# First convolution tap on ScalarE for 512 tokens of a tile, and the carried columns copied at the tile's head

## The chip, the cores and the metric

One core of a Trainium2 chip. The metric is the device time of one execution in microseconds: 3367.95 us, the median of three runs (3359.31, 3367.95 and 3372.1). Engines are called as in the profile: PE is TensorE, DVE is VectorE, ACT is ScalarE, POOL is GpSimd, SP is the queue that issues most DMAs.

## What is computed

One inference step of a decoder layer: projections, a state-space branch, attention over the prompt and over a paged cache, an output projection, and a feed-forward network with a causal depthwise convolution of width 3 on its gate branch. Only the last part matters here. For the 2048 tokens of the prompt:

```
gate = xn @ w_gate                      # 1024 -> 2816 channels
up   = xn @ w_up
padded = concatenate([conv_prev, gate]) # two earlier rows in front
conv = conv_b + sum(padded[:, i:i + t] * conv_w[i] for i in range(3))
hdn  = gelu(conv) * up
x    = x + rmsnorm(hdn @ w_down, g_post_ffn)
```

Eight sample tokens go through the same layer with a convolution state of their own. All data are float32.

## The kernel before, in words

**Tiles.** `stage_ffn` takes 128 of the 2816 channels and 1024 of the 2048 tokens at a time. That is 22 channel tiles for each half of the tokens, 44 tiles, called g = 0 to 43 here; g = 21 is the turn tile, in which the x operands of the second half are loaded and split, and from it on each tile also carries the eight sample tokens (`sample_channels`, `sample_taps`). Tiles 0 to 3 and 20 to 43 are written out; tiles 4 to 19 are a hardware loop of four passes with four tiles each, in which waits and addresses that depend on g go through registers.

**Seven products.** Gate and up for two times 512 tokens would be eight block products; the kernel makes them from seven, as in a Strassen-Winograd scheme, in the order K1, K6, K2, K7, K5, K4, K3. Each product is 12 matmuls of 128x512 (four blocks of x, three terms of a high and low part), so a tile is 84. They go into the PSUM banks A, B and C, and DVE and ACT add them up between: ACT copies K1 (L2852, tile `m1`) and K2 (L2858, into the first 512 tokens of `gbuf`, signal `c11_ready`); DVE makes L3058 after K6, L3063 after K7, L3066 after K5, L3069 after K4 and L3072 after K3. PE's product K7 waits for L3058, K4 for L3063, K3 for L3066. L3072 completes the other 512 tokens of `gbuf`.

**Weights.** For each product of the next tile ACT rounds the weight operand (L2798, `split`) and DVE makes its low part (L2949), both at the same step of the current tile. Four of the operands are sums that POOL makes first (L1736 to L1742). In every second tile of the loop POOL also makes four sums of x parts for the second half (L2642), on data that SP loads behind the stores of the pair.

**The convolution.** `taps` on DVE ends a tile. It copies the two columns carried from the previous token half, which are zeros in the first (L3017, signal `carried`), makes the first tap with the bias over all 1024 tokens (L3028), the two other taps (L3031, twice, signal `tapped`), and saves the last two columns (L3032, signal `saved`). Gelu of a tile (L2809, ACT) and the product with `up` (L2985, DVE) come at step K6 of the next tile. In even tiles DVE then adds the pair up (L2997) for SP to store; `w_down` is applied after the last tile (L2778).

**Order.** Each engine runs its list in the order written. The waits in front of the first tap guard its output `conv`: the stores and sums of the tiles that used that slot before, and in tiles 0 to 3, 22 and 23 the splits of x operands that are staged in the same memory.

Of the kernel before, what the change touches and what calls it, by code (L numbers as in the profile page):

```python
# [18 lines left out]
ALU = mybir.AluOpType  # L19
ACT = mybir.ActivationFunctionType  # L20
# [16 lines left out]
FT = FF // P  # L37
PAGE = 128
NPG = 64
CH = 512  # L40
GRP = 4
QUAD = P // GRP
CW = 3
ROWS = NS * (CW - 1) + CW + 1
TAP, BIAS = NS * (CW - 1), ROWS - 1
# [5 lines left out]
KH = KD // 2  # L51
OPS = 7
K1, K6, K2, K7, K5, K4, K3 = range(OPS)
# [2178 lines left out]
def stage_ffn(nc, A, keep, early):  # L2232

    with ExitStack() as ctx:
# [4 lines left out]
        PASS = 2 * CH  # L2239
# [61 lines left out]
        def xop(k, h):  # L2301
# [27 lines left out]
        sd_used, sd_upper, sd_summed, sd_placed = m.sem("sd_used"), m.sem("sd_upper"), m.sem("sd_summed"), m.sem("sd_placed")  # L2329
        s_squared, s_mean, s_r, s_scaled, s_y, s_x1, s_stored = (  # L2330
            m.sem(n) for n in ("s_squared", "s_mean", "s_r", "s_scaled", "s_y", "s_x1", "s_stored"))
        waited = m.sem("waited")

        def tiles(eng, body):

# [8 lines left out]
        def known(g, low, high=LASTG):  # L2344

            return isinstance(g, int) and low <= g < high

        def at(eng, sem, n):

            if not isinstance(n, int) or n > 0:  # L2350
                eng.wait_ge(sem, n)
# [66 lines left out]
        with nc.Block() as block:  # L2418
# [371 lines left out]
            def _(act):  # L2790
# [49 lines left out]
                def body(g, f, j, h2):  # L2840
                    s = j % 2
                    turn = known(g, FT - 1, FT)
                    sampled = known(g, FT - 1, LASTG - 1)
                    last = known(g, LASTG - 1)
                    for k in range(OPS):
                        if k == K1:
                            act.wait_ge(prod, g * OPS + k + 1)
                            at(act, c21_ready, g)
                            if known(g, 0, 1):
                                act.wait_ge(x_t4, 1)  # L2850
                                act.wait_ge(x_ready[K6], 1)
                            act.activation(m1, bank[:, 3 * s + A_B, :], ACT.Copy).then_inc(m1_ready, 1)  # L2852
                            if known(g, 0, 1):
                                split_q(K4, 2, x_t4, 1)
                        if k == K2:
                            act.wait_ge(prod, g * OPS + k + 1)
                            at(act, tapped, g * CW)
                            act.activation(gbuf[:, CW - 1:CW - 1 + CH], bank[:, 3 * s + A_B, :], ACT.Copy).then_inc(c11_ready, 1)  # L2858
                        if not last:
                            split(g + 1, k, (j + 1) % 2, h2 + j % 2)  # L2860
                        else:
                            if k == K7:
                                split_a(0)
                            for n in ((0, 1), (2,), (3, 4), (5, 6), (7, 8), (9, 10), ())[k]:
                                split_wd(n)
                            if k == K4:
                                split_a(1)
                        if k == K1 and sampled:
                            x = g - FT + 1
                            act.wait_ge(s_made, x + 1)  # L2870
                            at(act, s_ready, x)
                            act.activation(s_rows[:], bank[:, S_B, 0:2 * P].rearrange("p (q c) -> p q c", q=2), ACT.Copy).then_inc(s_copied, 1)
                        if k == K6 and not known(g, 0, 1):
                            gelu(g - 1, (j - 1) % 4)
                        if k == K5 and sampled:
                            act.wait_ge(s_tapped, (g - FT + 2) * CW)
                            act.activation(small[:], small[:], ACT.Gelu_apprx_tanh).then_inc(s_gelu, 1)
                        if turn:
                            for q in range(KH):
                                split_x(k, q)  # L2880
# [63 lines left out]
            def _(dve):  # L2944
# [67 lines left out]
                def taps(g, f, j, h2):  # L3012
                    one = lambda x: x[:, bass.ds(f, 1)].rearrange("p o n -> p (o n)")
                    p, tl, c = one(prm), one(tails), conv[:, j, :]
                    tap = lambda k: p[:, TAP + k:TAP + k + 1]
                    at(dve, saved, g)
                    ts(gbuf[:, 0:CW - 1], tl[:, 0:CW - 1], 1.0, None, ALU.mult).then_inc(carried, 1)  # L3017
                    dve.wait_ge(carried, g + 1)
                    dve.wait_ge(c11_ready, g + 1)
                    dve.wait_ge(c12_ready, g + 1)  # L3020
                    if not known(g, 0, 4):
                        dve.wait_ge(hraw_stored[j % 2], h2 * 16 - 16)
                        dve.wait_ge(hsummed, h2 * 5 - 5)
                    if known(g, 0, 4):
                        dve.wait_ge(x_ready[K4], 1)
                    if known(g, FT, FT + 2):
                        dve.wait_ge(x_ready[K3], 1 + KH)
                    ts(c, gbuf[:, 0:PASS], tap(0), p[:, BIAS:], ALU.mult, ALU.add).then_inc(tapped, 1)  # L3028
                    for k in (1, 2):
                        dve.wait_ge(tapped, g * CW + k)  # L3030
                        stt(c, gbuf[:, k:k + PASS], tap(k), c, ALU.mult, ALU.add).then_inc(tapped, 1)  # L3031
                    ts(tl[:, 0:CW - 1], gbuf[:, PASS:], 1.0, None, ALU.mult).then_inc(saved, 1)  # L3032
# [12 lines left out]
                def body(g, f, j, h2):  # L3045
                    b = lambda x: bank[:, 3 * (j % 2) + x, :]
                    turn = known(g, FT - 1, FT)
                    sampled = known(g, FT - 1, LASTG - 1)
                    last = known(g, LASTG - 1)
                    t1 = gbuf[:, CW - 1 + CH:]  # L3050
                    for k in range(OPS):
                        if k in (K6, K7, K5, K4, K3):
                            dve.wait_ge(prod, g * OPS + k + 1)
                        if k == K6:
                            dve.wait_ge(m1_ready, g + 1)
                            at(dve, tapped, g * CW)
                            at(dve, saved, g)
                            tt(t1, m1, b(B_B), ALU.add).then_inc(u2_ready, 1)  # L3058
                        if k == K7:
                            at(dve, h_ready, g)  # L3060
                            if known(g, 0, 1):
                                dve.wait_ge(x_t4, 1)
                            tt(up[:, CH:], m1, b(B_B), ALU.add).then_inc(u3_ready, 1)  # L3063
                        if k == K5:
                            dve.wait_ge(u3_ready, g + 1)
                            tt(up[:, CH:], up[:, CH:], b(C_B), ALU.add).then_inc(c22_ready, 1)  # L3066
                        if k == K4:
                            dve.wait_ge(c22_ready, g + 1)
                            tt(up[:, 0:CH], m1, b(B_B), ALU.add).then_inc(c21_ready, 1)  # L3069
                        if k == K3:  # L3070
                            dve.wait_ge(u2_ready, g + 1)
                            tt(t1, t1, b(C_B), ALU.add).then_inc(c12_ready, 1)  # L3072
                            if last:
                                split_wd(9)
                                split_wd(10)
                                split_a(1)
                            taps(g, f, j, h2)
                        if not last:
                            split(g + 1, k, (j + 1) % 2)
                        else:  # L3080
                            for n in ((0,), (1, 2), (3,), (4,), (5, 6), (7, 8), ())[k]:
                                split_wd(n)
                            if k == K5:
                                split_a(0)
                        if k == K6 and not known(g, 0, 1):
                            multiply(g - 1, (j - 1) % 4)
                        if j % 2 == 0 and not known(g, 0, 1):
                            sum_h(g, j, h2, {K2: (0, 1), K7: (2,), K5: (3,), K4: (4,)}.get(k, ()))
                        if k == K7 and sampled:
                            sample_taps(g - FT + 1)  # L3090
                        if k == K4 and sampled:
                            x = g - FT + 1
                            dve.wait_ge(s_gelu, x + 1)
                            tt(hs[:, x, 0:NS], small[:], bank[:, S_B, S_U:S_U + NS], ALU.mult).then_inc(s_h, 1)
                        if turn:
                            for q in range(KH):
                                split_x(k, q)
# [118 lines left out]
```

## Time and profile before

| what | value |
|---|---|
| median of three runs | 3367.95 us |
| the profiled execution: its time, its span | 3369.25 us, 3367.6 us |
| mean granted TensorE clock | 0.966 |
| PE busy over the span | 93% |
| DVE, ACT, POOL busy over the span | 71%, 39%, 28% |
| feed-forward tiles | from 1942 us to 2904 us of the span |

The span is the time from the first to the last instruction. A busy PE is one with matmuls in its pipeline. In the rows, a group of instructions is given by line, engine, operation, output and inputs; in a timeline the time in brackets is how long the engine was idle before it and which instruction ended that.

### The profile page before, as it was taken

To read this page: it belongs to the slowest core of one execution; us is meant where nothing else is said; L and a number is where in the kernel's file an instruction comes from. 1 tells how busy PE (TensorE), PEld (TensorE's weight loads), DVE (VectorE), ACT (ScalarE), POOL (GpSimd) and SP (SyncE) were. 2 spreads that over 40 slices of the span, in tenths; PEclk is the share of its full clock that TensorE was granted. 3 is DMA by queue.
4 is the path that set the end of the run, shared out by engine and by line. 5 is a ranking of instruction groups with operands and counts; after the bars stand their busy time and mean duration, and the time that the engine had idled before them with its cause. 6 is when DMAs were issued, how large, how long until landed. Compare 5 with 4: busy or idle time off the path is not lost. (4 is left out here: it accounts for less than half of the span.)

```text
span 3367.6 us, 46986 instructions
## 1 busy us (share of the span) xinstructions
PE 3115.7 (93%) x13945; PEld 2096.1 (62%) x13945; DVE 2377.6 (71%) x3069; ACT 1320.8 (39%) x2257; POOL 931.9 (28%) x823
## 2 busy tenths in 40 slices
PE   6999886899999999999889779999899999999998
PEld 5777663334344344344578557777677777787776
DVE  6111577998988988988546577777788888645565
ACT  5110112565566565565334333332423333332332
POOL 2000100643443443443034333333333333000001
PEclk8999988899999999999889889999999999999999
DMA  3331233979889889899555333444533333655564
GB/s 119 94 88 61 81 86 75 286 252 291 280 281 306 272 288 305 271 308 309 176 174 174 111 94 111 123 124 119 156 92 94 94 94 98 210 178 198 189 210 160
DMA packets 501234, 591.68 MB, mean 176 GB/s; under 512 B 66191, under 2 KB 308975, under 8 KB 499372
## 3 DMA queue, kind: packets, MB, share of 16 engines
q1 hardware_dynamic: 494094, 574.17, 54.7%
q10 hardware_dynamic: 6912, 15.26, 1.4%
q8 instruction: 75, 1.23, 0.2%
q14 instruction: 121, 0.99, 0.1%
q0 software_dynamic: 32, 0.03, 0.0%
HBM read 484.37 MB, written 103.86 MB: 175 GB/s over the span
## 5 line engine op out<-in xcount | busy, mean ns | idle before, releaser
L2701 PE MATMUL tail_bank<-rounded_xw,rounded_wop 128*128 128x512 f32 x2112 | 515.4, 401 | 44.3 <-DVE rounded_xw L2954 31.4
L2701 PEld LDWEIGHTS tail_bank<-rounded_xw,rounded_wop 128*128 128x128 f32 x2112 | 398.6, 191 | 148.0 <-issue 50.1
L1378 POOL TENSOR_TENSOR att_S<-att_S,att_X 128x512 f32<-128x512 f32 (+3 forms) x256 | 345.3, 1349 | 284.4 <-PE att_bank L1667 221.9
L2701 PE MATMUL tail_bank<-gate_xr,rounded_wop 128*128 128x512 f32 x1584 | 380.8, 397 | 18.5 <-DVE gate_work L3063 17.2
L2778 PE MATMUL tail_bank<-rounded_xw,rounded_wop 128*128 128x512 f32 x1488 | 357.3, 396 | 0.0
L2701 PEld LDWEIGHTS tail_bank<-gate_xr,rounded_wop 128*128 128x128 f32 x1584 | 297.9, 189 | 94.4 <-DVE rounded_wop L2949 17.3
L1562 DVE TENSOR_TENSOR att_prod<-att_Kr,att_q_wide 128x1024 f32<-128x1024 f32 x256 | 326.5, 1275 | 5.4 <-DMA att_Kr<-in_cache_k_dram 5.3
L2778 PEld LDWEIGHTS tail_bank<-rounded_xw,rounded_wop 128*128 128x128 f32 x1488 | 278.3, 188 | 77.9 <-issue 11.7
L1662 PE MATMUL att_bank<-att_X,att_negtri 128*128 128x512 f32 (+3 forms) x640 | 298.9, 549 | 29.3 <-DVE att_X L1533 28.7
L1567 DVE TENSOR_REDUCE att_z_s<-att_prod 128x16 f32<-128x1024 f32 x256 | 313.3, 1224 | 8.8
L1428 ACT ACTIVATE att_X<-att_bank 128x512 f32<-128x512 f32 (+2 forms) x320 | 171.2, 535 | 256.1 <-PE att_bank L1651 222.3
L1667 PE MATMUL att_bank<-att_S,att_negones 128*128 128x512 f32 (+3 forms) x576 | 258.6, 531 | 0.0
L2798 ACT ACTIVATE rounded_wop<-ahead_wf 128x512 fp32r<-128x512 f32 x215 | 134.2, 628 | 264.5 <-PE tail_bank L2701 235.7
L1436 ACT ACTIVATE att_Wt<-att_bank 128x512 f32<-128x512 f32 (+2 forms) x320 | 168.8, 527 | 127.8 <-PE att_bank L1667 127.5
L1533 DVE SCALAR_TENSOR_TENSOR att_X<-att_X,att_bank 128x512 f32<-128x512 f32 (+2 forms) x320 | 191.2, 599 | 28.4 <-ACT att_X L1430 27.2
L1651 PEld LDWEIGHTS att_bank<-att_qhh,att_khl 128*128 128x128 f32 x320 | 61.0, 191 | 217.7 <-ACT att_Wt L1436 139.7
L1667 PEld LDWEIGHTS att_bank<-att_S,att_negones 128*128 128x128 f32 x576 | 111.8, 194 | 121.4 <-issue 106.3
L1430 ACT ACTIVATE att_X<-att_X 128x512 f32<-128x512 f32 (+2 forms) x320 | 181.3, 567 | 10.2
L1374 POOL TENSOR_TENSOR att_S<-att_X,att_zero 128x128 f32<-128x128 f32 x120 | 98.8, 824 | 292.4 <-PE att_bank L1667 179.5
L1682 PE MATMUL att_bank<-att_Wt,att_vh 128*64 128x512 f32 (+3 forms) x640 | 161.0, 560 | 7.4 <-ACT att_Wt L1436 7.4
L2949 DVE TENSOR_TENSOR rounded_wop<-ahead_wf,rounded_wop 128x512 fp32r<-128x512 f32 x215 | 157.3, 747 | 12.8 <-ACT rounded_wop L2798 11.4
L1651 PE MATMUL att_bank<-att_qhh,att_khl 128*128 128x512 f32 (+2 forms) x320 | 156.4, 489 | 1.4 <-ACT att_Wt L1436 0.8
(426 smaller groups left out, 5472.1 us busy)
## 6 DMA issues: line engine op xcount, KB each, us to landing
att_Kr<-in_cache_k_dram SPq DMA_DIRECT2D x512, 256.0 KB, 3.8
att_Vr<-in_cache_v_dram SPq DMA_DIRECT2D x488, 256.0 KB, 3.9
hop_dram<-gate_work SPq DMA_DIRECT2D x154, 256.0 KB, 2.7
ffn_xw_raw<-in_w_down_dram SPq DMA_DIRECT2D x109, 256.0 KB, 5.5
ahead_wf<-hop_dram SPq DMA_DIRECT2D x38, 704.0 KB, 4.2
ahead_wf<-in_w_gate_dram SPq DMA_DIRECT2D x44, 512.0 KB
ahead_wf<-in_w_up_dram SPq DMA_DIRECT2D x44, 512.0 KB, 5.4
down_a_far<-hop_dram SPq DMA_DIRECT2D x18, 704.0 KB, 4.3
```

Source lines behind the costliest of these rows:

```text
L1378: pool.tensor_tensor(new[:, r:], old[:, r:], x[:, r:], ALU.add).then_inc(s_part, 1)
L1428: act.activation(x, bank[:, s % NZ, cols(s):], ACT.Exp).then_inc(e_ready, 1)
L1430: act.activation(x, x, ACT.Ln, bias=1.0).then_inc(l_ready, 1)
L1436: act.activation(Wt[:, u % NW, cols(u):], bank[:, u % NZ, cols(u):], ACT.Exp).then_inc(w_ready, 1)
L1533: stt(x, x, LN_TOP, z, ALU.min, ALU.max).then_inc(sp_ready, 1)
L1562: tt(pr, Kr[:, kk % KSLOTS], q_wide[:, None, :].to_broadcast([P, PP, AW]), ALU.mult).then_inc(k_used, 1)
L1567: dve.tensor_reduce(z_s[:, :, kk * PP:(kk + 1) * PP].rearrange("p h r -> p r h"), prod[:, kk % 2, :].rearrange("p (k h d) -> p k h d", k=P ...
L1651: mm = pe.matmul(bank[:, s % NZ, o:], key[:, j * P:(j + 1) * P], part[:, c * CH + o:(c + 1) * CH], start=(q == 0), stop=(q == 1))
L1662: last = pe.matmul(bank[:, u % NZ, o:], negtri[:], X[:, u % NX, o:], start=False, stop=True, skip_group_check=True)
L1667: last = pe.matmul(bank[:, u % NZ, o2:], negones[:], S[:, (u - 1) % 2, o2:], start=False, stop=True, skip_group_check=True)
L2701: mm = pe.matmul(bank[:, b, :], wop[:, k, w, q], xop(k, x)[:, q], start=(k in (K1, K6, K5) and q == 0 and n == 0), stop=(q == KH - 1 and n ...
L2778: mm = pe.matmul(bank[:, s % 3, :], a_op[s % 2][a][:, p, :], wd_op[n % NW][:, w], start=(p == 0 and q == 0), stop=(p == PAIRS_F - 1 and q ...
```

## The change

For the first 512 tokens of a tile the first tap is made by ACT, directly after its copy of K2, with the taps' weight as scale and the bias as bias. The waits that guard `conv` are repeated in front of it on ACT. DVE makes the first tap for the other 512 tokens only and waits for ACT's signal `half_tapped` before the second tap. The copy of the carried columns moves from `taps` to the head of the tile, step K1, in DVE's list.

```
--- before.py
+++ after.py
@@ -2329,7 +2329,7 @@
         sd_used, sd_upper, sd_summed, sd_placed = m.sem("sd_used"), m.sem("sd_upper"), m.sem("sd_summed"), m.sem("sd_placed")
         s_squared, s_mean, s_r, s_scaled, s_y, s_x1, s_stored = (
             m.sem(n) for n in ("s_squared", "s_mean", "s_r", "s_scaled", "s_y", "s_x1", "s_stored"))
-        waited = m.sem("waited")
+        half_tapped, waited = m.sem("half_tapped"), m.sem("waited")
 
         def tiles(eng, body):
 
@@ -2856,6 +2856,18 @@
                             act.wait_ge(prod, g * OPS + k + 1)
                             at(act, tapped, g * CW)
                             act.activation(gbuf[:, CW - 1:CW - 1 + CH], bank[:, 3 * s + A_B, :], ACT.Copy).then_inc(c11_ready, 1)
+                            if not known(g, 0, 4):
+                                act.wait_ge(hraw_stored[j % 2], h2 * 16 - 16)
+                                act.wait_ge(hsummed, h2 * 5 - 5)
+                            if known(g, 0, 4):
+                                act.wait_ge(x_ready[K4], 1)
+                            if known(g, FT, FT + 2):
+                                act.wait_ge(x_ready[K3], 1 + KH)
+                            act.wait_ge(carried, g + 1)
+                            act.wait_ge(c11_ready, g + 1)
+                            p = prm[:, bass.ds(f, 1)].rearrange("p o n -> p (o n)")
+                            act.activation(conv[:, j, 0:CH], gbuf[:, 0:CH], ACT.Identity, scale=p[:, TAP:TAP + 1], bias=p[:, BIAS:]
+                                           ).then_inc(half_tapped, 1)
                         if not last:
                             split(g + 1, k, (j + 1) % 2, h2 + j % 2)
                         else:
@@ -3013,9 +3025,6 @@
                     one = lambda x: x[:, bass.ds(f, 1)].rearrange("p o n -> p (o n)")
                     p, tl, c = one(prm), one(tails), conv[:, j, :]
                     tap = lambda k: p[:, TAP + k:TAP + k + 1]
-                    at(dve, saved, g)
-                    ts(gbuf[:, 0:CW - 1], tl[:, 0:CW - 1], 1.0, None, ALU.mult).then_inc(carried, 1)
-                    dve.wait_ge(carried, g + 1)
                     dve.wait_ge(c11_ready, g + 1)
                     dve.wait_ge(c12_ready, g + 1)
                     if not known(g, 0, 4):
@@ -3025,7 +3034,8 @@
                         dve.wait_ge(x_ready[K4], 1)
                     if known(g, FT, FT + 2):
                         dve.wait_ge(x_ready[K3], 1 + KH)
-                    ts(c, gbuf[:, 0:PASS], tap(0), p[:, BIAS:], ALU.mult, ALU.add).then_inc(tapped, 1)
+                    ts(c[:, CH:], gbuf[:, CH:PASS], tap(0), p[:, BIAS:], ALU.mult, ALU.add).then_inc(tapped, 1)
+                    dve.wait_ge(half_tapped, g + 1)
                     for k in (1, 2):
                         dve.wait_ge(tapped, g * CW + k)
                         stt(c, gbuf[:, k:k + PASS], tap(k), c, ALU.mult, ALU.add).then_inc(tapped, 1)
@@ -3049,6 +3059,10 @@
                     last = known(g, LASTG - 1)
                     t1 = gbuf[:, CW - 1 + CH:]
                     for k in range(OPS):
+                        if k == K1:
+                            at(dve, saved, g)
+                            ts(gbuf[:, 0:CW - 1], tails[:, bass.ds(f, 1), 0:CW - 1].rearrange("p o n -> p (o n)"), 1.0, None, ALU.mult
+                               ).then_inc(carried, 1)
                         if k in (K6, K7, K5, K4, K3):
                             dve.wait_ge(prod, g * OPS + k + 1)
                         if k == K6:
```

## Rows read from the trace of the kernel before

**Rows 1.** Windows, second half of the stage: window, its us, busy us of each engine, clock, DMA.

```profile
2443.00:2881.00 438.00, 438.00 (x2131) 342.24 (x2131) 372.06 (x530) 137.79 (x245) 151.27 (x81) 1.00 0.34 93
```

**Rows 2.** Line L2701, the tiles' matmuls: what ended PE's idle time, us in total, times.

```profile
  DVE gate_work L3063: 17.2, 10
```

**Rows 3.** Timeline of DVE at tile 6's end: start us, us, engine, line, operation.

```profile
2104.69 0.69 DVE L3072 TENSOR_TENSOR gate_work<-gate_work,tail_bank 128x512 f32<-128x512 f32 x1 [0.84 <-PE tail_bank L2701]
2105.30 0.16 DVE L3017 TENSOR_SCALAR gate_work<-ffn_tails 128x2 f32 x1
2105.93 0.81 DVE L3028 TENSOR_SCALAR gate_work<-gate_work,ahead_prm 128x1024 f32<-128x1024 f32 x1 [0.47 <-DVE gate_work L3017]
2106.89 2.72 DVE L3031 SCALAR_TENSOR_TENSOR gate_work<-gate_work,ahead_prm 128x1024 f32<-128x1024 f32 x2
```

**Rows 4.** Timeline of the stopped tile 7, four engines.

```profile
2108.86 4.53 POOL L2642 TENSOR_TENSOR ffn_stage<-ffn_stage 128x256 f32<-128x256 f32 x4 [11.68 <-DMA ffn_stage<-xnT_dram]
...
2116.13 0.63 ACT L2798 ACTIVATE rounded_wop<-ahead_S 128x512 fp32r<-128x512 f32 x1 [7.52 <-POOL ahead_S L1738]
...
2117.62 0.58 ACT L2858 ACTIVATE gate_work<-tail_bank 128x512 f32<-128x512 f32 x1
...
2118.10 1.14 ACT L2798 ACTIVATE rounded_wop<-ahead_wf 128x512 fp32r<-128x512 f32 x2
2119.01 0.68 DVE L2949 TENSOR_TENSOR rounded_wop<-ahead_wf,rounded_wop 128x512 fp32r<-128x512 f32 x1
...
2119.61 0.67 DVE L3063 TENSOR_TENSOR gate_work<-gate_work,tail_bank 128x512 f32<-128x512 f32 x1
...
2120.43 5.84 PE L2701 MATMUL tail_bank<-gate_xr,rounded_wop 128*128 128x512 f32 x24 [1.78 <-DVE gate_work L3063]
```

**Rows 5.** Timeline of the even tile 8, where PE doesn't stop.

```profile
2135.28 0.62 ACT L2798 ACTIVATE rounded_wop<-ahead_wf 128x512 fp32r<-128x512 f32 x1
...
2135.93 0.69 DVE L2949 TENSOR_TENSOR rounded_wop<-ahead_wf,rounded_wop 128x512 fp32r<-128x512 f32 x1 [0.95 <-ACT rounded_wop L2798]
...
2137.30 8.56 PE L2701 MATMUL tail_bank<-gate_xr,rounded_wop 128*128 128x512 f32 x36
...
2138.85 0.68 DVE L3063 TENSOR_TENSOR gate_work<-gate_work,tail_bank 128x512 f32<-128x512 f32 x1
...
2145.70 11.36 PE L2701 MATMUL tail_bank<-rounded_xw,rounded_wop 128*128 128x512 f32 x48
```

**Rows 6.** Timeline of tile 5: the last tap of tile 4 and POOL's sums.

```profile
2067.13 1.28 DVE L3031 SCALAR_TENSOR_TENSOR gate_work<-gate_work,ahead_prm 128x1024 f32<-128x1024 f32 x1 [0.15 <-DVE gate_work L3031]
2068.29 3.92 POOL L2642 TENSOR_TENSOR ffn_stage<-ffn_stage 128x256 f32<-128x256 f32 x4 [12.34 <-DMA ffn_stage<-xnT_dram]
```

**Rows 7.** Activations elsewhere: a timeline in attention, and a group with busy us, mean ns.

```profile
999.89 0.60 ACT L1428 ACTIVATE att_X<-att_bank 128x512 f32<-128x512 f32 x1 [1.14 <-PE att_bank L1651]
1000.52 0.63 ACT L1430 ACTIVATE att_X<-att_X 128x512 f32<-128x512 f32 x1
...
L1406 ACT ACTIVATE att_qlb<-att_wide,att_bias_now 64x512 fp32r<-64x512 f32 x32 | 23.0, 718 | 0.8
```

**Rows 8.** Timeline of the even tile 42, second half.

```profile
2868.87 0.60 ACT L2858 ACTIVATE gate_work<-tail_bank 128x512 f32<-128x512 f32 x1 [1.16 <-PE tail_bank L2701]
...
2871.91 3.43 PE L2701 MATMUL tail_bank<-gate_xr,rounded_wop 128*128 128x512 f32 x14
...
2872.99 0.67 DVE L3063 TENSOR_TENSOR gate_work<-gate_work,tail_bank 128x512 f32<-128x512 f32 x1
```

**Rows 9.** Timeline of the turn: first tap of tile 21, PE in tile 22.

```profile
2433.94 1.86 DVE L3028 TENSOR_SCALAR gate_work<-gate_work,ahead_prm 128x1024 f32<-128x1024 f32 x1
...
2442.82 4.58 PE L2701 MATMUL tail_bank<-rounded_xw,rounded_wop 128*128 128x512 f32 x12 [3.56 <-DVE rounded_wop L2949]
```

**Rows 10.** Timeline behind the last tile: PE starts the second product with w_down.

```profile
2922.36 0.97 PE L2778 MATMUL tail_bank<-rounded_stage,rounded_wop 128*128 128x512 f32 x3 [2.15 <-DVE rounded_wop L2978]
```

**Rows 11.** Groups of ACT's instructions: the table load ahead of the stage.

```profile
L2827 ACT ACT_TABLE_LOAD x1 | 1.3, 1283 | 6.6 <-PEq L67 6.6
```

More of the change, by code:

```diff
@@ L2331, in stage_ffn @@
             m.sem(n) for n in ("s_squared", "s_mean", "s_r", "s_scaled", "s_y", "s_x1", "s_stored"))
-        waited = m.sem("waited")
+        half_tapped, waited = m.sem("half_tapped"), m.sem("waited")
         def tiles(eng, body):
@@ L2858, in body @@
                             act.activation(gbuf[:, CW - 1:CW - 1 + CH], bank[:, 3 * s + A_B, :], ACT.Copy).then_inc(c11_ready, 1)
+                            if not known(g, 0, 4):
+                                act.wait_ge(hraw_stored[j % 2], h2 * 16 - 16)
+                                act.wait_ge(hsummed, h2 * 5 - 5)
+                            if known(g, 0, 4):
+                                act.wait_ge(x_ready[K4], 1)
+                            if known(g, FT, FT + 2):
+                                act.wait_ge(x_ready[K3], 1 + KH)
+                            act.wait_ge(carried, g + 1)
+                            act.wait_ge(c11_ready, g + 1)
+                            p = prm[:, bass.ds(f, 1)].rearrange("p o n -> p (o n)")
+                            act.activation(conv[:, j, 0:CH], gbuf[:, 0:CH], ACT.Identity, scale=p[:, TAP:TAP + 1], bias=p[:, BIAS:]
+                                           ).then_inc(half_tapped, 1)
                         if not last:
@@ L3015, in taps @@
                     tap = lambda k: p[:, TAP + k:TAP + k + 1]
-                    at(dve, saved, g)
-                    ts(gbuf[:, 0:CW - 1], tl[:, 0:CW - 1], 1.0, None, ALU.mult).then_inc(carried, 1)
-                    dve.wait_ge(carried, g + 1)
                     dve.wait_ge(c11_ready, g + 1)
@@ L3027, in taps @@
                         dve.wait_ge(x_ready[K3], 1 + KH)
-                    ts(c, gbuf[:, 0:PASS], tap(0), p[:, BIAS:], ALU.mult, ALU.add).then_inc(tapped, 1)
+                    ts(c[:, CH:], gbuf[:, CH:PASS], tap(0), p[:, BIAS:], ALU.mult, ALU.add).then_inc(tapped, 1)
+                    dve.wait_ge(half_tapped, g + 1)
                     for k in (1, 2):
@@ L3051, in body @@
                     for k in range(OPS):
+                        if k == K1:
+                            at(dve, saved, g)
+                            ts(gbuf[:, 0:CW - 1], tails[:, bass.ds(f, 1), 0:CW - 1].rearrange("p o n -> p (o n)"), 1.0, None, ALU.mult
+                               ).then_inc(carried, 1)
                         if k in (K6, K7, K5, K4, K3):
```

## The prediction

> **What bounds the kernel now.** I read the page first: the change touches the feed-forward stage, 44 tiles numbered 0 to 43 from 1942 us to 2904 us of the span. By windows, TensorE (PE) is busy for all of 438 us in the second half of that stage, tiles 22 to 42 [rows 1], so nothing that DVE or ACT saves there can shorten anything; it can only get longer. In the first half PE does stop: the line of its matmuls lists 17.2 us of waiting for DVE L3063, in 10 places [rows 2]. In order of time, eight of the ten are in the odd tiles 5 to 19 and look like the one below, one is in the turn tile 21 and one in the last tile. Only these stops, the turn of the halves (2402 to 2443 us) and the end of the stage can move.
>
> A stopped tile, number 7: GpSimd (POOL) makes four sums on tile parts from 2108.86, then the weight sums of the next tile; ACT rounds the K6 operand at 2116.13 as soon as they are there, does gelu, then copies the K2 product (L2858) at 2117.62 and rounds the K2 operand at 2118.10; DVE makes the low part of that operand at 2119.01, then L3063 at 2119.61; PE starts K4 at 2120.43, 0.15 us behind L3063's end [rows 4]. It had been idle for 1.78 us. ACT, which is otherwise mostly idle, is a link of the only chain that stops PE, and the new instruction goes into that link.
>
> **What the change adds on ACT.** One activation of 128x512 per tile, SBUF to SBUF, scale and bias each read per partition, between L2858 and the rounding of the K2 operand. The trace has no such form. Nearest from below: an activation SBUF to SBUF of this size with a constant bias, 0.63 us, starting 0.03 us behind the end of the one whose result it reads. Nearest from above: a 64x512 copy with a scale per partition, 0.718 us [rows 7]. There is one per-partition operand more here; I take 0.75, bounds 0.63 and 0.85 (0.718 plus, once more and a half, the 0.09 between the two rows).
>
> ScalarE: Activation LUTs, section What ACT_TABLE_LOAD costs, of the Trainium skill, gives 186 ns plus 0.833 ns a column plus about 93 ns for each per-partition operand: 0.80 us as an estimate. The rows have 0.63 for one operand less than 0.718, so they agree in the step and not quite in the base; by the page the forecast would be about 1 us later.
>
> The K2 rounding now starts 0.48 us after L2858 starts, which is L2858's 0.58 less 0.10 of overlap [rows 4]. With the tap between, it starts 0.58 + 0.03 + L - 0.10, so it is delayed by L + 0.03 = 0.78. In the 16 looped tiles (4 to 19) waits and operands go by registers: DVE sat 0.47 us before L3028 there, waiting for its own two-column copy [rows 3]. On ACT most of this can be done while L2858 runs; I take 0.10 of it (bounds 0 and 0.44) and have 0.88. None of the five new waits on ACT should hold: the stores and sums they ask for are those of two or more tiles ago, and the carried copy is made at the head of the same tile. Behind them on ACT is the K2 rounding and, through it, DVE's low part, POOL's fourth weight sum and L3063.
>
> Odd tiles 5 to 19: DVE took the K2 operand at 2119.01, while ACT's rounding (0.62 us, as at 2135.28 [rows 5]) was done by 2118.72; 0.25 of the delay is hidden by DVE's multiply, so L3063 and PE are later by 0.63 each.
>
> Even tiles 4 to 18: DVE waits for ACT already (0.95 us idle, start at 2135.93), then has two sums and L3063, ending 2139.53. PE started K5 at 2137.30; 36 matmuls take until the next row's start at 2145.70, so twelve take 2.80 and K4 would come at 2140.10. Less the 0.15, the slack is 0.42 [rows 5]. The delay of 0.88 eats it and leaves a new stop of 0.46. Tiles 2 and 20 have the same order, outside the loop: 0.36 each.
>
> Second half, even tiles: L3063 ends at 2873.66, PE takes K4 2.80 us after 2871.91, less 0.15, that is 2874.56 [rows 8]. The slack is 0.90, the delay 0.78 at most: nothing, but with only 0.12 to spare. Odd tiles there have no sums and far more room.
>
> **What it takes from DVE.** The first pass at the tile's end shrinks from 1024 to 512 columns: 0.81 us against 0.16 for two columns, so 0.49 for half, 0.32 saved; and the two-column copy with its wait leaves the place between L3072 (end 2105.38) and L3028 (2105.93) [rows 3]. A wait for L3072's own result stays; I take 0.30 for it in the loop. The passes of L3031 then start and end 0.57 earlier (bounds 0.3 and 0.8). The copy itself is only moved, to a place behind which DVE waits for the K6 operand, in tile 7 from about 2112.6 to 2116.8. What this buys: POOL's four sums took 3.92 us in tile 5, where the last L3031 ended at 2068.41, 0.12 into them, and 4.53 in tile 7, where it ended at 2109.61, 0.75 into them [rows 3, 4, 6]. 0.61 us for 0.63 of overlap: one for one, down to no overlap. So POOL, and the chain behind it, gains about 0.50 in each of the eight stopped tiles (bounds 0.1 and 0.6, for the moved two-column copy now lies in these sums). This is the one way in which the change can pay in this stretch. In the second half both run together as well, but PE waits for neither.
>
> **Sum over the first half.** A pair of tiles: +0.46 (even) + 0.63 (odd) - 0.50 = 0.59 us; eight pairs 4.7; tiles 2 and 20 0.7; together +5.4.
>
> The turn: the x operands are loaded behind DVE's end of tile 20, 0.3 earlier; PE sat 3.56 us until 2442.82 behind a DVE that ran without a gap from the taps of tile 21, whose first pass took 1.86 beside POOL [rows 9]. Half a pass and the moved copy give back 1.2 or so; ACT's tap of tile 21 lies in a stretch where it also splits x and costs 0.2 net. I take -1.3, bounds -2.5 and +0.5. In tile 22 ACT must wait for the last x split (staged where the tap writes), a wait of some 2 us, but DVE, which makes those splits, comes to the K2 operand only three instructions later.
>
> The end: taps 42 and 43 each lead to a transfer that PE waits for, the second one with a stop of 2.15 us [rows 10]. Minus 0.5 each, plus 0.5 for the tap on ACT ahead of the last w_down roundings: -0.5, bounds -1.0 and +0.5.
>
> Total +5.4 - 1.3 - 0.5 = +3.6 us on the profiled execution, 3369.25 us (span 3367.6 and 1.65 around it): 3372.85. The median of the runs shown is 1.3 below the profiled one, so 3371.6: **3372 us**.
>
> **Rivals.** First, the gains win: tap at 0.63, no register cost, delay 0.66; even +0.24, odd +0.41, POOL -0.55, so 0.10 a pair; 0.8 + 0.5 - 2.5 - 1.0 = -2.2 us, about 3366. For it: DVE is the busier engine. Against: PE does not wait for DVE's sum of work, it waits for one chain.
>
> Second, slower than before: the tap turns the ACT link into a stop in every looped tile. Price: tap 0.80 and the full 0.44 of registers make the delay 1.27; even 0.85, odd 1.02, POOL only -0.20: 1.67 for each of eight pairs, 13.4; tiles 2 and 20 0.8; nothing back at the turn and the end: +14.2, about 3382. It decides from a delay of 0.42 on in even and 0.25 in odd tiles; past 0.90 the ten even tiles of the second half begin to stop as well, and a tap of 1.1 us would add 2 us more. For it: DVE's 0.47; against: that was a wait on its own result just before.
>
> In the same direction, ScalarE: Activation LUTs, Rules for kernel authors, of the Trainium skill says that multiply and add belong on VectorE. The rows agree on engine time: 0.63 to 0.85 on ACT to save 0.32 on DVE.
>
> Third, the tap needs a table that gelu's set has not: two loads a tile, 1.283 us each [rows 11], delay 3.35 to 3.45. Eight pairs at 5.7, tiles 2 and 20 at 2.9, ten even tiles of the second half at 2.4: about +75 us, 3444. The copies and gelu alternate all through the stage without a load, but a copy is not an affine map. The same page of the Trainium skill (section Table sets) puts identity into every set, which speaks against this one; no row of this trace shows that function.
>
> Chances: forecast 0.72, gains win 0.14, ACT link 0.12, table 0.02. A measurement of this kernel tells about 0.5% (17 us) from no change; the first two cases and most of the third lie inside. Faster by more is next to excluded, since all ten stops together are 17.2 us: 0.03. Slower by more is the table and a dear third case: 0.08. Same 0.89. The range takes both middle cases and the 12.8 us between the three runs of before: 3359 to 3384.
>
> **What the profile after will show.** Right: PE's idle time by L3063 rises from 17.2 to about 22 us, in about 20 places instead of 10, the new ones of about half a microsecond in even tiles; in odd tiles about 2 us; POOL's four sums at about 3.9 us; the new ACT activation at 0.7 to 0.8 us; PE busy for all of tiles 22 to 42; DVE busy shorter by some 14 us (44 times 0.32) without a use. Wrong: no new stops in even tiles (then the tap is cheaper or overlapped), stops in the second half (the 0.12 was not there), any table load in the stage, or a stop of ACT in front of the tap of over 0.5 us outside tile 22.

## The result, and the profile after

The changed kernel takes 3386.07 us (median of six runs, 3382.63 to 3395.57) against 3370.98 us for the kernel before in the same comparison: ratio 1.0053, interval 1.0041 to 1.0065. It is slower by 18 us, 14 to 22 by the interval. The forecast was 3372 with a range up to 3384.

The profiled execution of each kernel can be cut at two points: PE's first matmul of the stage (L2701) and its first matmul for the samples (L2715), which opens tile 21.

| us | before | after |
|---|---|---|
| up to the first matmul of tile 0 | 1942.6 | 1942.7 |
| from there to tile 21 | 450.3 | 473.5 |
| from there to the end of the span | 974.7 | 974.1 |
| span | 3367.6 | 3390.3 |

All of the loss lies in tiles 0 to 20. This is line L2701 of the changed kernel again, what ended PE's idle time, us in total and times. L3077 is the old L3063, L3072 the old L3058 and L2961 the old L2949. The line counts PE's weight loads too: 22.3 of the 31.1 us for L2961 are theirs and fall into the same eight odd stops as the matmuls' waits for L3077, so they are not a loss of their own. The row for L3072 is the turn.

```profile
  DVE rounded_wop L2961: 31.1, 12
  DVE gate_work L3077: 26.2, 20
  DVE gate_work L3072: 8.5, 1
```

Against 17.2 us in 10 places [rows 2], there are 26.2 in 20. PE's timeline of the changed kernel shows both kinds of stop, and something that no sum of stops holds:

```profile
2103.53 5.83 PE L2701 MATMUL tail_bank<-gate_xr,rounded_wop 128*128 128x512 f32 x24 [0.55 <-DVE gate_work L3077]
2109.20 11.36 PE L2701 MATMUL tail_bank<-rounded_xw,rounded_wop 128*128 128x512 f32 x48
2120.40 2.96 PE L2701 MATMUL tail_bank<-gate_xr,rounded_wop 128*128 128x512 f32 x12
2125.70 7.38 PE L2701 MATMUL tail_bank<-gate_xr,rounded_wop 128*128 128x512 f32 x24 [2.33 <-DVE gate_work L3077]
```

Tile 6 has one of the forecast's new stops, 0.55 us. Tile 7's stop has grown from 1.78 [rows 4] to 2.33, and the 24 matmuls behind it take 7.38 us where the same 24 took 5.84 before. The windows over these groups, of the changed kernel and then of the one before (window, its us, busy us of PE, weight loads, DVE, ACT and POOL, granted clock, DMA):

```profile
2125.70:2132.90 7.20, 7.20 (x24) 5.75 (x25) 4.90 (x5) 0.63 (x1) 4.55 (x4) 0.76 0.00 0
2147.62:2153.20 5.58, 5.58 (x24) 4.52 (x25) 4.82 (x8) 0.76 (x2) 0.00 (x0) 1.00 0.48 141
```

```profile
2120.43:2126.10 5.67, 5.67 (x24) 4.59 (x25) 3.80 (x5) 0.63 (x1) 3.69 (x4) 1.00 0.00 0
```

The granted clock is 0.76 behind the stop of 2.33 us, that is, it was at the lower of its two levels (1.2 GHz of 2.4) for part of the group, and 1.00 behind the short stop of tile 8 and behind the 1.78 of before. From the start of such a group to the next tile it is 7.22 us instead of 5.67: 1.55 us lost. It happens in seven of the eight odd tiles from 5 to 19. Below, a group is called slow when it is at the lower clock for part of its time, as this one.

The link on ACT in tile 7, changed kernel (answers to [rows 3, 4]):

```profile
2110.53 0.55 DVE L3037 TENSOR_SCALAR gate_work<-gate_work,ahead_prm 128x512 f32<-128x512 f32 x1 [0.45 <-DVE gate_work L3086]
2111.23 2.71 DVE L3041 SCALAR_TENSOR_TENSOR gate_work<-gate_work,ahead_prm 128x1024 f32<-128x1024 f32 x2 [0.15 <-DVE gate_work L3037]
...
2113.60 4.17 POOL L2642 TENSOR_TENSOR ffn_stage<-ffn_stage 128x256 f32<-128x256 f32 x4 [11.37 <-DMA ffn_stage<-xnT_dram]
...
2115.08 0.70 DVE L3064 TENSOR_SCALAR gate_work<-ffn_tails 128x2 f32 x1
...
2120.50 0.63 ACT L2798 ACTIVATE rounded_wop<-ahead_S 128x512 fp32r<-128x512 f32 x1 [7.18 <-POOL ahead_S L1738]
...
2121.99 0.58 ACT L2858 ACTIVATE gate_work<-tail_bank 128x512 f32<-128x512 f32 x1
...
2122.89 0.82 ACT L2869 ACTIVATE gate_work<-gate_work,ahead_prm 128x512 f32<-128x512 f32 x1 [0.32 <-ACT gate_work L2858]
2123.61 1.13 ACT L2798 ACTIVATE rounded_wop<-ahead_wf 128x512 fp32r<-128x512 f32 x2
2124.26 0.69 DVE L2961 TENSOR_TENSOR rounded_wop<-ahead_wf,rounded_wop 128x512 fp32r<-128x512 f32 x1 [0.82 <-ACT rounded_wop L2798]
2124.87 0.68 DVE L3077 TENSOR_TENSOR gate_work<-gate_work,tail_bank 128x512 f32<-128x512 f32 x1
```

The K2 rounding now starts 1.62 us after L2858 starts, against 0.48: a delay of 1.14. POOL's four sums take 4.17 us instead of 4.53 in this tile, the largest gain of the eight; on the mean of the odd tiles 5 to 19 they take 4.20 instead of 4.39.

The loss in tiles 0 to 20, item by item: ten even stops, 4.9 us of idle time in all, each with 0.16 of late start that the idle time does not show, 6.5 us; eight odd stops grown from 14.0 to 19.05 us, 5.0; seven slow groups of 1.55, 10.9. Together 22.4 of 23.2 us. Most of the other 0.8 lies behind the even stops: the 24 matmuls after one take 5.67 us to the next tile, where the same 24 take 5.60 in a row that doesn't stop (two thirds of 8.40 for 36), so ten times 0.07.

### The profile page after: what moved, and what is told of

It is laid out like the page before. It is cut to its first block and busy times, and to the rows that moved or that the text cites. A ratio compares the mean times of both kernels' runs of the same rounds, so it can differ in the third digit from the quotient of the medians.

```text
span 3390.3 us, 47172 instructions
## 1 busy us (share of the span) xinstructions
PE 3132.4 (92%) x13945; PEld 2102.9 (62%) x13945; DVE 2368.0 (70%) x3069; ACT 1356.8 (40%) x2301; POOL 920.0 (27%) x823
## 5 line engine op out<-in xcount | busy, mean ns | idle before, releaser
L2701 PE MATMUL tail_bank<-rounded_xw,rounded_wop 128*128 128x512 f32 x2112 | 515.4, 401 | 44.1 <-DVE rounded_xw L2966 31.4
L2701 PEld LDWEIGHTS tail_bank<-rounded_xw,rounded_wop 128*128 128x128 f32 x2112 | 398.2, 190 | 147.6 <-issue 49.8
L2701 PE MATMUL tail_bank<-gate_xr,rounded_wop 128*128 128x512 f32 x1584 | 393.2, 405 | 27.6 <-DVE gate_work L3077 26.2
L2701 PEld LDWEIGHTS tail_bank<-gate_xr,rounded_wop 128*128 128x128 f32 x1584 | 303.5, 193 | 110.6 <-DVE rounded_wop L2961 22.3
L2961 DVE TENSOR_TENSOR rounded_wop<-ahead_wf,rounded_wop 128x512 fp32r<-128x512 f32 x215 | 161.1, 751 | 56.4 <-ACT rounded_wop L2798 55.3
```

Of the source, the lines that this page charges most:

```text
L2701: mm = pe.matmul(bank[:, b, :], wop[:, k, w, q], xop(k, x)[:, q], start=(k in (K1, K6, K5) and q == 0 and n == 0), stop=(q == KH - 1 and n ...
```

## The experiments

The theory: the tap sits in ACT's list ahead of the K2 rounding, on the chain to L3063; its delay makes new stops and longer ones, and the long ones cost PE its clock as well. The rivals: the loss comes from the tap being on ACT at all, or from DVE's side (the moved copy, its use of memory beside POOL's sums); and the lower clock has another cause than the length of the stop. "Stretch" is the time from the first matmul to tile 21 in the profiled execution. Ratios are to the kernel before. The stops and groups of the table are those behind L3063 (L3077, L3078 or L3065 in the other kernels) in tiles 1 to 20.

| kernel | ratio (interval) | stretch | odd stops, us each | slow groups | even stops |
|---|---|---|---|---|---|
| before | 1 | 450.3 | 1.72 to 1.78 | 0 of 8 | none |
| after | 1.0053 (1.0041 to 1.0065) | 473.5 | 2.33 to 2.64 | 7 of 8 | 10, 4.9 us |
| e1 tap behind | 0.9983 (0.9973 to 0.9992) | 448.2 | 1.42 to 1.75 | 0 of 8 | none |
| e2 ACT part alone | 1.0071 (1.0057 to 1.0085) | 477.3 | 2.66 to 2.75 | 8 of 8 | 10, 4.9 us |
| e3 DVE part alone | 0.9985 (0.9975 to 0.9996) | 448.5 | 1.42 to 2.03 | 0 of 8 | none |
| e4 256 tokens | 1.0048 (1.0034 to 1.0062) | 469.7 | 2.27 to 2.55 | 6 of 8 | 8, 2.7 us |
| e5 POOL order, before | 0.9962 (0.9948 to 0.9976) | 437.4 | none | none | none (odd: 6, 1.6 us, L3058) |
| e6 POOL order, after | 0.9969 (0.9956 to 0.9982) | 441.8 | none | none | 10, 4.9 us |
| e7 POOL order, tap behind | 0.9930 (0.9913 to 0.9947) | 434.5 | none | none | none |
| e8 copy at head | 0.9998 (0.9986 to 1.0010) | 454.7 | 1.81 to 1.86 | 2 of 8 | none |

**e1: the tap behind the rounding.** The tap with all its waits (the last of them shown) moves down in ACT's list, nothing else:

```
                             act.activation(gbuf[:, CW - 1:CW - 1 + CH], bank[:, 3 * s + A_B, :], ACT.Copy).then_inc(c11_ready, 1)
...
-                            act.wait_ge(c11_ready, g + 1)
...
-                            act.activation(conv[:, j, 0:CH], gbuf[:, 0:CH], ACT.Identity, scale=p[:, TAP:TAP + 1], bias=p[:, BIAS:]
...
                         if not last:
                             split(g + 1, k, (j + 1) % 2, h2 + j % 2)
...
+                        if k == K2:
...
+                            act.wait_ge(c11_ready, g + 1)
...
+                            act.activation(conv[:, j, 0:CH], gbuf[:, 0:CH], ACT.Identity, scale=p[:, TAP:TAP + 1], bias=p[:, BIAS:]
...
```

> As the changed kernel, but ACT makes the tap behind its K2 rounding instead of ahead of it. Theory (the tap's place in ACT's list delays the K2 operand, so L3063, so PE; and stops that grow past 2 us cost PE its clock too): no stop in even tiles, the eight odd ones at 1.4 us (1.78 less the 0.36 that POOL's sums gained), no matmul group at the lower clock, the gain of 1.7 us at the stage's end kept: 3 to 5 us faster than before, ratio 0.9985 to 0.9995. Rival (the tap costs by being on ACT at all, or the moved copy and its port use do it): still 12 to 18 us slower, ratio 1.004 to 1.005.

Measured: 0.9983, 6 us faster than before. That is a little more than the theory's 0.9985 to 0.9995 (the interval, 0.9973 to 0.9992, covers most of it) and 18 us off the rival's. ACT still makes the tap, DVE is still relieved, the copy is still at the head; only the place differs from the changed kernel. Tile 7 of this kernel:

```profile
2113.29 0.58 ACT L2858 ACTIVATE gate_work<-tail_bank 128x512 f32<-128x512 f32 x1
...
2113.76 0.62 ACT L2798 ACTIVATE rounded_wop<-ahead_wf 128x512 fp32r<-128x512 f32 x1
2114.28 0.80 ACT L2879 ACTIVATE gate_work<-gate_work,ahead_prm 128x512 f32<-128x512 f32 x1
2114.68 0.68 DVE L2962 TENSOR_TENSOR rounded_wop<-ahead_wf,rounded_wop 128x512 fp32r<-128x512 f32 x1
...
2116.11 5.83 PE L2701 MATMUL tail_bank<-gate_xr,rounded_wop 128*128 128x512 f32 x24 [1.48 <-DVE gate_work L3078]
```

The tap, 0.80 us here, now runs while DVE makes the low part, and in tiles 1 to 20 PE stops no longer than in the kernel before. One item of the expectation failed: the gain at the stage's end was not kept. The last tile's stop is 2.22 us and the group behind it slow, as in the kernel before; e9 and e10 below show that this end differs between executions of one kernel.

**e2: the ACT part alone.** The changed kernel with DVE's first tap over all tokens:

```
-                    ts(c[:, CH:], gbuf[:, CH:PASS], tap(0), p[:, BIAS:], ALU.mult, ALU.add).then_inc(tapped, 1)
                    dve.wait_ge(half_tapped, g + 1)
+                    ts(c, gbuf[:, 0:PASS], tap(0), p[:, BIAS:], ALU.mult, ALU.add).then_inc(tapped, 1)
```

> The ACT half of the change alone: ACT makes the tap in the changed kernel's place and the copy is at the tile's head, but DVE still makes the first tap for all 1024 tokens, over it. Theory: DVE saves nothing, so POOL gains less; stops of 2.5 to 2.7 us in odd tiles and 0.55 in even ones, the lower clock behind every odd stop: 20 to 27 us slower than before, ratio 1.006 to 1.008. Rival (DVE's shorter work is what collides with POOL and brings the loss): no slower than before by more than 5 us.

Measured: 1.0071, 24 us slower, with the ten even stops of the changed kernel and a slow group behind each of the eight odd ones. The copy at the head is in this kernel too, but e8 shows no difference from it alone. So the ACT part carries the whole loss; DVE's shorter work is what softens it.

**e3: the DVE part alone.** No tap on ACT; the first tap of the first 512 tokens is left out. The edit, against the changed kernel:

```
-                            act.activation(conv[:, j, 0:CH], gbuf[:, 0:CH], ACT.Identity, ...).then_inc(half_tapped, 1)
...
-                    dve.wait_ge(half_tapped, g + 1)
+                    dve.wait_ge(carried, g + 1)
```

> The DVE half alone: DVE makes the first tap for tokens 512 to 1023 only and the copy is at the head; ACT makes no tap, so the first tap of the first 512 tokens is left out. Theory: POOL's four sums at 4.2 us instead of 4.5, stops of 1.4 us in odd tiles, none in even ones, PE always at the higher clock in the stage: 3 to 6 us faster, ratio 0.998 to 0.999. Rival (the moved copy or the new contention costs): 5 us or more slower.

Measured: 0.9985, 5 us faster, stretch 448.5. That is what e1 reached with the tap made, so behind the rounding the tap costs nothing that can be measured. The whole gain of DVE's shorter work is 2 us in this stretch: seven of the eight odd stops shrink by about 0.3 each, while the first, in tile 5, is 2.03 us instead of 1.78.

**e4: 256 tokens.** `gbuf[:, 0:CH // 2]` on ACT, `CH // 2` to the end on DVE.

> As the changed kernel, but ACT taps 256 tokens and DVE 768. By the rows the tap takes 0.60 us instead of 0.82, so the K2 operand is later by 0.93 instead of 1.14: stops of 0.33 in even tiles and about 2.1 in odd ones. Theory that the clock goes with the length of the stop: groups at the lower clock in some or none of the odd tiles, 5 to 10 us slower than before (1.0015 to 1.003). Rival that the lower clock does not hang on the stop's length: seven slow groups as in the changed kernel, 14 to 16 us slower (1.004 to 1.005).

Measured: 1.0048, 16 us slower, which the ranges gave to the rival. The trace shows why the range missed. Even stops are 0.33 as expected. Odd stops are 2.27, not 2.1: in tile 7 the K6 operand was rounded 0.16 us later in the tile than in the changed kernel (POOL's sums took as long, 4.19 and 4.17, but started 0.14 later), which takes back most of the 0.21 that the shorter tap gives. And at 2.27 the clock mostly falls:

```profile
2166.58 7.38 PE L2701 MATMUL tail_bank<-gate_xr,rounded_wop 128*128 128x512 f32 x24 [2.27 <-DVE gate_work L3077]
...
2210.40 5.83 PE L2701 MATMUL tail_bank<-gate_xr,rounded_wop 128*128 128x512 f32 x24 [2.27 <-DVE gate_work L3077]
```

The first group is slow; the second, behind the same stop, is not. I had set the length at which the clock falls too high. This run alone could not have told length from chance.

**e5: another order on POOL.** The odd stops existed before. POOL's sums of x parts move behind the first three weight sums:

```
                        prepare(g + 1, (j + 1) % 2, h2 + j % 2)
+                    if i is not None and j % 2 == 1:
+                        sum_parts(i, j // 2)
...
-                    if i is not None and j % 2 == 0:
-                        sum_parts(i, j // 2)
```

> The kernel before, with POOL's four sums of x parts made behind the first three weight sums of the next tile instead of ahead of them (nothing else moves). Theory (the eight odd stops come from the K6 operand waiting for POOL): these stops of 1.95 us are gone, 13 to 16 us faster than before, ratio 0.995 to 0.996. Rival (the stops come from DVE or from the loads and only show behind POOL): stops stay, within 5 us of before.

Measured: 0.9962, 13 us faster, at the edge of the range. The odd stops are gone, as the theory had it. Six small stops of 0.24 to 0.28 us came in their place, waiting for L3058. Probably DVE gets there later because POOL's sums now lie beside more of its work; that was not tried by itself.

```profile
2153.93 3.04 PE L2701 MATMUL tail_bank<-rounded_xw,rounded_wop 128*128 128x512 f32 x12 [0.24 <-DVE gate_work L3058]
```

**e6: the same order in the changed kernel.**

> The changed kernel with the same new order on POOL. Theory: odd stops gone and with them every matmul group at the lower clock; the ten even stops (PE late by 0.4 to 0.7 us) stay, the gain of 1.7 us at the stage's end too: 8 to 11 us faster than the kernel before and 4 to 6 us slower than the one that has the new order alone, ratio 0.997. Rival (the lower clock comes from the tap in some other way than through the odd stops): slow groups stay, no faster than before.

Measured: 0.9969, 10 us faster than before, and 441.8 us in the stretch, 4.4 more than e5 (the medians, 3359.24 and 3356.44, are 2.8 apart). No slow group is left in the stretch and the ten even stops are those of the changed kernel to 0.01 us. So in the stretch the lower clock comes with the long stop and not with the tap, and the even stops are the tap's own. The gain at the stage's end failed here too: a last stop of 2.79 us with a slow group behind it.

**e7: POOL's order and the tap behind the rounding.**

> New order on POOL and ACT's tap behind its K2 rounding. Theory: no stop in tiles 1 to 20 at all, the end's gain kept: 15 to 19 us faster than before, ratio 0.9945 to 0.9955, the best of all; 1 to 4 us faster than the new order alone. Rival (once POOL's stops are gone the tap gives nothing): the same as the new order alone within 1 us.

Measured: 0.9930 (median 3343.72 us), 24 us faster than before and the fastest of all, more than the 15 to 19 expected. PE does not stop once between tile 1 and tile 21, here in tiles 7 and 8:

```profile
2089.79 8.33 PE L2701 MATMUL tail_bank<-gate_xr,rounded_wop 128*128 128x512 f32 x35
2097.95 11.36 PE L2701 MATMUL tail_bank<-rounded_xw,rounded_wop 128*128 128x512 f32 x48
2109.16 8.56 PE L2701 MATMUL tail_bank<-gate_xr,rounded_wop 128*128 128x512 f32 x36
```

The stretch is 434.5, 15.8 under before and 2.9 under e5: relieving DVE pays here because it removes e5's six stops for L3058. The rest of the 24 us, some 8 us, lies ahead of the stage and from tile 21 on, and no run explains it: the interval alone gives 18 to 29 us, and over all profiles the stage began anywhere from 1930.4 to 1946.0 us. The end's gain was not kept, as in e1 and e6 (last stop 2.23 us, slow group).

**e8: the copy at the head alone.** DVE's copy moves to step K1, all else as before.

> The kernel before with the copy of the carried columns at the tile's head only; DVE makes the first tap for all tokens, ACT none. Theory: the passes of L3031 start about 0.2 us earlier, POOL's sums gain 0.1 to 0.2 us: 0 to 3 us faster, ratio 0.999 to 1.000. Rival (the two-column copy beside POOL's sums takes what it gives): 0 to 3 us slower.

Measured: 0.9998, no difference; the interval covers both expectations. The odd stops are longer by 0.09 on the mean and the profiled stretch by 4.4 us, 3.1 of it from two slow groups, which is the rival's sign: the copy lands beside POOL's sums, where a two-column copy takes 0.70 us (L3064 above) instead of 0.16. And the first of these stops shows how near the kernel before already was:

```profile
2072.12 7.38 PE L2701 MATMUL tail_bank<-gate_xr,rounded_wop 128*128 128x512 f32 x24 [1.85 <-DVE gate_work L3065]
```

**e9, e10, e11: how fixed is the lower clock?** The changed kernel twice more and the kernel before once more, one profile each.

> The changed kernel once more, one profile. Theory (a stop over 2 us usually, not always, drops PE's clock, 1.55 us each): the same stops to within 0.05 us, but another number or other places of slow groups among the eight odd tiles; the stretch from the first matmul to tile 21 is 473.5 us less 1.55 for each slow group fewer than seven. Rival (the lower clock is tied to a place in the program): the same seven groups, 473.5 us again.

> The same as the look before: the theory expects the stretch at 473.5 us less 1.55 us for each slow group fewer than seven, with the places moving from one execution to another; the rival the same seven places.

> The kernel before once more, one profile: stops of 1.72 to 1.78 us in the eight odd tiles. Theory: no slow group or one, the stretch from the first matmul to tile 21 at 450.3 us (452 with one). Rival (slow groups come by chance whatever the stop): several of them, 455 us or more.

Measured: the changed kernel has seven slow groups in both, and 473.5 and 473.4 us in the stretch, so the number did not move. The place did: tile 19 was spared in the first profile and in e10, tile 17 in e9:

```profile
2300.26 7.37 PE L2701 MATMUL tail_bank<-gate_xr,rounded_wop 128*128 128x512 f32 x24 [2.35 <-DVE gate_work L3077]
...
2344.36 5.83 PE L2701 MATMUL tail_bank<-gate_xr,rounded_wop 128*128 128x512 f32 x24 [2.35 <-DVE gate_work L3077]
...
2386.92 7.37 PE L2701 MATMUL tail_bank<-gate_xr,rounded_wop 128*128 128x512 f32 x24 [2.35 <-DVE gate_work L3077]
```

The kernel before has none again, stretch 450.3. All profiles together, odd tiles 5 to 19 only: behind stops of 1.42 to 1.78 us 0 of 31 groups were slow, at 1.81 to 1.86 two of 8, at 2.03 none of one, at 2.27 to 2.29 five of 7, at 2.33 to 2.66 in the changed kernel and e4 22 of 25, and 8 of 8 in e2.

Outside these tiles the length of the stop decides less. Behind the last tile's stop the group was slow after 2.00 to 2.33 us in six profiles (before, e1, e5, e7, e8, e11) and after 2.79, 3.05 and 3.25 us (e6, e4, e2), not slow after 1.45 and 1.55 us (after, e3), and also not after 3.13 and 3.35 us, in e9 and e10. This is e9's; its granted clock over 2917.59 to 2923.20 is 1.00:

```profile
2917.59 5.84 PE L2701 MATMUL tail_bank<-gate_xr,rounded_wop 128*128 128x512 f32 x24 [3.13 <-DVE gate_work L3077]
```

So a longer stop makes the lower clock likely in the looped tiles, but length alone is not the condition. What else decides was not tried; nor was a stop above 2.03 us in an odd tile without the even stops beside it, so a part of the even stops in it is not excluded, though e8 had two slow groups without any.

## Why the prediction was wrong

**What held.** The place was right: PE's stops for L3063, nowhere else. Ten new even stops came, the odd ones grew, tiles 22 to 42 stayed without a stop (barely: outside the loop the K2 rounding came later by 0.94, not "0.78 at most", which used up the slack of 0.90, and in the even tiles there 36 matmuls took about 8.62 us instead of 8.56), no table load appeared, and ACT's wait in tile 22 (1.77 us) did no harm. The rival "the ACT link turns into a stop in every looped tile" was the right description, and I gave it 0.12.

**The step that failed most: "Total +5.4 - 1.3 - 0.5", a sum of idle times only.** It took every matmul to run at the same speed, whatever stood before it. I saw that the stops of 1.78 us would become longer and never asked what PE does after a longer one. The seven slow groups are 10.9 us, nearly half of the loss, and the slow rival's 3382 lacked them too. Of the 17.8 us by which the first half missed +5.4, they are 10.9; the even stops, with the matmuls behind them, are 2.8 and the odd ones 4.0. The kernel before shows the case, and I had not weighed it. Behind the last tile's stop of 2.11 us, the same 24 matmuls take 7.38, and the row of the turn that the forecast used [rows 9] has 12 matmuls in 4.58 us behind 3.56 of idle time, where twelve take 3.04 behind a short stop (2153.93 above).

```profile
2896.58 7.38 PE L2701 MATMUL tail_bank<-gate_xr,rounded_wop 128*128 128x512 f32 x24 [2.11 <-DVE gate_work L3063]
```

TensorE: Matmul & The Clock Gate, Part 1, of the Trainium skill says that the array's clock drops to half when PE has been idle and comes back once it is busy; the granted clock of 0.76 agrees, and this rule would have been the one to weigh. The last tiles of e9 and e10, at 1.00 behind more than 3 us, show that not every idle time does it.

**"I take 0.75" and "I take 0.10 of it".** The tap took 0.816 us in the median of 44, and in the loop it started 0.32 behind L2858's end instead of 0.03 + 0.10. The 0.44 bound was nearer than my guess that it runs in L2858's shadow. The delay in the loop is 1.14, not 0.88. With it the even stops of the loop make PE late by 0.71 instead of 0.46. ScalarE: Activation LUTs (What ACT_TABLE_LOAD costs) of the Trainium skill had 0.80 for the tap and was the better estimate.

**"One for one, down to no overlap."** POOL's sums gained 0.20 on the mean of the eight tiles and 0.36 in tile 7, not 0.50. A slope taken from two tiles held in sign only: DVE's first tap for 512 tokens took 0.55 rather than 0.49 and waited 0.45 instead of 0.30 in front, and a second two-column copy of 0.70 now lies beside the sums (L3064, next to the one that saves the last columns). How much of the shortfall is whose was not tried. DVE's busy time over the span fell by 9.6 us, not 14. So tile 7 became late by 0.55 more (2.33 against 1.78), an odd tile on the mean by 0.63, where the forecast had 0.63 - 0.50 = 0.13.

**"L3063 and PE are later by 0.63 each."** This assumed 0.25 hidden by DVE's multiply, which it was: 1.14 less 0.25 is 0.89. From the K6 rounding, which POOL releases, to L3077 it is 4.37 us (2120.50 to 2124.87) where it was 3.48 (2116.13 to 2119.61 [rows 4]), and that is 0.89 more. The step was right; the delay put into it was too small.

**The turn and the end.** From tile 21's first matmul to PE's restart in tile 22 it is 49.7 us instead of 50.0: -0.2, not -1.3. The first tap did shrink there (0.75 for 1.86), but L3086, in front of it, came 1.3 us later in the tile than L3072 had, behind two x splits that took 3.39 us. In e9 and e10 L3086 was not late and the restart came at 49.3 and 49.1, against 50.5 in e11. So the direction was right, and one profile can't tell the size. The end gave -1.6 in the profile of the changed kernel, more than -0.5, but not in the way forecast: the group behind the last stop stayed at the higher clock. This is the changed kernel's:

```profile
2919.64 5.84 PE L2701 MATMUL tail_bank<-gate_xr,rounded_wop 128*128 128x512 f32 x24 [1.45 <-DVE gate_work L3077]
```

The stop of 1.45 us is no gain of the change either: the same kernel has 3.13 and 3.35 there in e9 and e10. From tile 21 to the end of the span the three profiles of the changed kernel take 974.1, 972.1 and 973.0 us, the two of the kernel before 974.7 and 974.8. That is 0.6 to 2.7 less, where the forecast had 1.8: near it, but by luck as to the end, since its terms did not come true one by one.

**The range** ended at 3384 because the "price" of the slow rival was made of the same kind of terms as the forecast. The profiled executions differ by 22.7 us, the timed ones by 14 to 22.

## What to carry to other kernels

An instruction that is moved to an idle engine is not free if it stands in front of one that the bottleneck waits for: ask for the next instruction in that engine's list, and put the new one behind it (e1 against the changed kernel: 25 us in one stretch, with the same instructions). When a wait of the bottleneck grows, price also what it does after the wait: here 0.55 us more of a stop mostly cost 1.55 us more of matmuls. Take more than one profile before a gain of 1 or 2 us in one place is put down to a change: the changed kernel's last stop was 1.45, 3.13 and 3.35 us in three executions. And the stop that a change lengthens is often worth removing itself: another order on POOL gave 13 us in the stretch, the relief of DVE 2.

## What the runs showed of the hardware that was not expected

- In the looped tiles the granted clock fell behind stops of PE as short as 1.81 us (2 of 8 in e8) and in 30 of 33 cases behind 2.33 us or more; in the last tile it stayed at 1.00 behind 3.13 and 3.35 us (e9, e10). When it falls, it costs 1.55 us for 24 matmuls of 512 columns here, three times the growth of the stop that brought it.
- In the hardware loop, ACT's tap, whose waits and addresses are in registers there, starts 0.32 us after its operand is there (16 times, 5.2 us in all); outside the loop the same tap starts 0.12 us behind (2014.07, after L2858's end at 2013.95).
- A two-column DVE copy takes 0.70 us while POOL's sums run (2115.08 above), against 0.16 us without them [rows 3].
